# Short-row weights and tables laid out with 16 KB per partition, the last up matrix in quarters, and every second unit of expert weights issued by ScalarE's queue

## What is computed

```python
def hierarchical_moe(h, wg_r, bg_r, we_r, be_r, w_gate, w_up, w_down):
    """Top-1 expert group, then top-2 experts inside it; SwiGLU experts."""
    ...
    def expert_block(args):
        xb, e = args
        a = jax.nn.silu(xb @ w_gate[e]) * (xb @ w_up[e])
        return a @ w_down[e]
```

## Time and profile before

| | us |
|---|---|
| median of three runs | 1203.53 |
| the profiled execution | 1203.57 |
| its span in the trace | 1201.8 |
| TensorE busy | 961.0 |
| VectorE busy | 212.3 |
| ScalarE busy | 140.9 |

### The profile page before, as it was taken

The page is one execution under the profiler, slowest core; times in us unless marked ns, Lnnn a source line. Parts: engine busy times, 40 slices in busy tenths (PEclk is TensorE's granted clock), DMA queues, the critical chain, the costliest instruction groups (busy, mean ns, idle before and its releaser), DMA issues.

```text
span 1201.8 us, 11705 instructions
## 1 busy us (share of the span) xinstructions
PE 961.0 (80%) x5158; PEld 409.9 (34%) x5158; DVE 212.3 (18%) x457; ACT 140.9 (12%) x263; POOL 10.2 (1%) x11
## 2 busy tenths in 40 slices
PE   8999999867676767685789999997676767676758
PEld 7655554221212222222236655532121212121312
DVE  3812332010101010100025541410000000000101
ACT  3411211000000000000021330110000000000001
POOL 0000010000000000000000000000000000000000
PEclk9999999987878887888899999997878887878879
DMA  9772498999999999999997327999999999999996
GB/s 341 227 303 105 157 417 355 429 428 427 428 428 429 428 428 428 427 427 428 416 387 297 141 86 322 376 429 428 429 426 427 428 429 427 428 428 428 429 420 269
DMA packets 63237, 447.29 MB, mean 372 GB/s; under 512 B 13136, under 2 KB 13392, under 8 KB 40656
## 3 DMA queue, kind: packets, MB, share of 16 engines
q1 hardware_dynamic: 63184, 446.49, 90.0%
HBM read 445.43 MB, written 1.05 MB: 372 GB/s over the span
## 4 chain that ended last, share of the span: by engine, by line
DMA 50%; PE 47%; DVE 1%; ACT 1%; issue 0%; SPq 0%; DVEq 0%
PE psum L568 18%; DMA ring<-in_w_up 13%; PE psum L918 11%; DMA wide<-in_w_down 10%; DMA wide<-in_w_gate 10%; DMA ring<-in_w_down 5%; DMA wide<-in_w_up 5%; DMA ring<-in_w_gate 5%; PE psum L915 5%; PE psum L978 5%; PE psum L516 1%; PE psum L504 1%; DMA ring<-in_w_in_ab 1%; PE psum L992 1%; PE psum L636 0%
## 5 line engine op out<-in xcount | busy, mean ns | idle before, releaser
L568 PE MATMUL psum<-ring,mixed 128*32 128x512 f32 x1664 | 406.0, 712 | 125.5 <-DMA ring<-in_w_up 59.0
L568 PE MATMUL psum<-wide,mixed 128*32 128x512 f32 x1376 | 394.6, 709 | 101.2 <-DMA wide<-in_w_gate 61.9
L568 PEld LDWEIGHTS psum<-ring,mixed 128*32 128x32 f32 x1664 | 91.5, 128 | 331.7 <-issue 163.8
L568 PEld LDWEIGHTS psum<-wide,mixed 128*32 128x32 f32 x1376 | 87.2, 127 | 256.5 <-issue 116.3
L918 PE MATMUL psum<-ring,wide 128*128 128x512 f32 x320 | 140.5, 593 | 1.3 <-DVE wide L830 1.3
L918 PEld LDWEIGHTS psum<-ring,wide 128*128 128x128 f32 x320 | 59.7, 191 | 69.5 <-issue 67.8
L504 PE MATMUL psum<-y_sb,spread 128*128 128x512 f32 x144 | 67.2, 607 | 2.8 <-ACT y_sb L695 1.4
L752 DVE TENSOR_TENSOR mixed<-psum,sig 128x512 f32<-128x512 f32 x16 | 16.9, 1058 | 280.7 <-PE psum L568 280.7
L516 PEld LDWEIGHTS psum<-sel,h 128*128 128x128 f32 x528 | 60.5, 192 | 17.0 <-issue 15.1
L516 PE MATMUL psum<-sel,h 128*128 128x128 f32 x528 | 64.3, 279 | 1.7 <-DVE sel L728 1.7
L678 ACT COPY mixed<-psum 128x512 f32<-128x512 f32 x34 | 19.7, 586 | 344.7 <-PE psum L516 344.7
(11 more groups left out here) (252 smaller groups left out, 505.4 us busy)
## 6 DMA issues: line engine op xcount, KB each, us to landing
ring<-in_w_down SPq DMA_DIRECT2D x38, 2048.0 KB, 34.8
ring<-in_w_up SPq DMA_DIRECT2D x36, 2048.0 KB, 37.8
wide<-in_w_gate SPq DMA_DIRECT2D x34, 2048.0 KB, 37.2
ring<-in_w_gate SPq DMA_DIRECT2D x30, 2048.0 KB, 30.6
wide<-in_w_up SPq DMA_DIRECT2D x28, 2048.0 KB, 27.1
wide<-in_w_down SPq DMA_DIRECT2D x24, 2048.0 KB, 35.5
ring<-in_w_in_ab SPq DMA_DIRECT2D x8, 2048.0 KB, 14.3
ring<-in_w_in_cd SPq DMA_DIRECT2D x6, 2048.0 KB, 20.5
```

Of the source, the lines that this page charges most:

```text
L568: mm = pe.matmul(psum[slots, out + n, :], inp[:, c, slots], slot(layer, unit)[:, at + 512 * n:at + 512 * (n + 1)], start=c == 0, stop=c == ...
```

## The change

The input weights, output weights, quartered matrices and small tables are rearranged before the launch, so that every 2 MB unit is read as one 16 KB row per partition, and all small tables but two gains (and `positions`) as one array `tables` of 1188 floats per partition. Quad 7's up matrix joins `QUARTERED`. Units 11, 13, 15 ... 83 of each layer's experts leave SP's stream and are issued from ScalarE's, by `load_more`, after the sigmoid, after the copy of the transposed routing weights and after the output copy; for this ScalarE's loop over the quads is written out. Units 84 to 95 stay with SP. The diff's core:

```diff
-N_SMALL = 19
+N_SMALL = 2
...
-QUARTERED = ((0, 0), (QUADS - 1, 2))
+QUARTERED = ((0, 0), (QUADS - 1, 1), (QUADS - 1, 2))
...
+        def load_unit(eng, layer, n, dst_cols, src):
+            if unit_free(layer, n):
+                eng.wait_ge(S["unit_used"], unit_free(layer, n))
+            eng.dma_start(dst_cols(slot(layer, n)), src).then_inc(unit_landed[unit_place(layer, n)], 16)
...
+            elif (quad, matrix) in QUARTERED:
+                load_unit(eng, layer, expert_unit(layer, u), lambda s: s, t["quarters"][layer, matrix, j])
...
+        def from_act(u):
+
+            return len(PLACES_MOE) <= u < n_moe - PER_QUAD and u % 2 == 1
...
             def load_in(layer, n):
-                b = BLOCKS[layer][n]
-                src = w_in[layer][0].rearrange("(c p) n -> p c n", p=P)[:, :, b * 512:(b + 1) * 512]
-                load_unit(layer, n, lambda s: s.rearrange("p (c n) -> p c n", c=KC), src)
+                load_unit(sp, layer, n, lambda s: s, t["w_in"][layer * UNITS_IN[0] + n])
...
+            sp.dma_start(tables[:, :], t["tables"]).then_inc(S["lb_landed"], 16)
...
                 for u in range(10, n_moe):
-                    load_expert_unit(layer, u)
+                    if not from_act(u):
+                        load_expert_unit(sp, layer, u)
...
+            def load_more(i, matrices):
+
+                if over:
+                    return
+                freed = moe_base(layer) + i * PER_QUAD + matrices * TILE
+                for u in range(n_moe):
+                    if from_act(u) and freed - TILE < unit_free(layer, expert_unit(layer, u)) <= freed:
+                        load_expert_unit(act, layer, u)
+
             def act_quad(i, last=False):
                 wait_matrices(act, layer, rnd, i, 1)
                 nc.scalar.activation(sig, psum[:, GATE, :], ACT.Sigmoid).then_inc(m["sig_ready"], 1)
+                load_more(i, 1)
                 keep_gathered(i + (n17 + 2))
                 act.wait_ge(m["turned"], n16 + i + 1)
                 nc.scalar.copy(actT, psum[:, GATE, :].rearrange("p (c s) -> p c s", c=FC))
                 nc.scalar.copy(spread, psum[:, UP, 0:TC * P].rearrange("p (c s) -> p c s", c=TC)).then_inc(m["actT_ready"], 1)
+                load_more(i, 2)
...
                 nc.scalar.copy(y_sb[:, 0:512], psum[:, YB, :]).then_inc(m["y_ready"], 1)
+                load_more(i, 3)
```

More of the change, by code:

```diff
@@ L331, in heads, with load_expert_unit @@
             return a.rearrange("p c (h d) -> p c h d", h=HEADS)
+        def load_unit(eng, layer, n, dst_cols, src):
+            if unit_free(layer, n):
+                eng.wait_ge(S["unit_used"], unit_free(layer, n))
+            eng.dma_start(dst_cols(slot(layer, n)), src).then_inc(unit_landed[unit_place(layer, n)], 16)
+        def load_expert_unit(eng, layer, u):
+            quad, matrix, j = u // PER_QUAD, u // TILE % MATRICES, u % TILE
+            w, rows = (("w_gate", KC), ("w_up", KC), ("w_down", FC))[matrix]
+            if u == n_moe - 1:
+                n = expert_unit(layer, u)
+                eng.wait_ge(S["unit_used"], unit_free(layer, n))
+                for b, signal in enumerate((S["half_landed"], unit_landed[unit_place(layer, n)])):
+                    eng.dma_start(slot(layer, n)[:, b * HALF:(b + 1) * HALF],
+                                 t["quarters"][layer, 2, j, :, b * HALF:(b + 1) * HALF]).then_inc(signal, 16)
+            elif (quad, matrix) in QUARTERED:
+                load_unit(eng, layer, expert_unit(layer, u), lambda s: s, t["quarters"][layer, matrix, j])
+            else:
+                src = t[w][layer, quad * TILE + j].rearrange("(p c) n -> p (c n)", c=rows)
+                load_unit(eng, layer, expert_unit(layer, u), lambda s: s, src)
@@ L346, in load_expert_unit @@
[L346 to L364, removed]
@@ L413, in _ @@
+            for which, name in enumerate(("ret_gnorm", "hgrn_onorm")):
+                sp.dma_start(retg[:, which, :], t[name].rearrange("a h d -> a (h d)").broadcast_to([P, GROUP_W])).then_inc(
+                    S["small_landed"], 16)
             for layer in range(2):
@@ L697, in moe_act @@
             keep_gathered(n17 + 1, first=not over)
[L698 to L701, removed]
+            if over:
+                with act.Fori(0, QUADS) as i:
+                    act_quad(i)
+            else:
+                for i in range(QUADS):
+                    act_quad(i, last=i == QUADS - 1)
         def clear_outputs(layer):
@@ L1794, in _, with laid_out, quarters @@
             add_experts(dve, 1)
[L1797 to L1800, removed]
+PARAMS = ["x", "norm_ffn", "ret_gnorm", "hgrn_onorm", "w_gate", "w_up", "w_down"]
+def laid_out(inputs):
+    put = {n: np.ascontiguousarray(inputs[n]) for n in PARAMS}
+    w_in, w_out = [], []
+    for layer, pair in enumerate(("ab", "cd")):
+        for b in BLOCKS[layer]:
+            block = inputs["w_in_" + pair][0][:, b * 512:(b + 1) * 512]
+            w_in.append(block.reshape(KC, P, 512).transpose(1, 0, 2).reshape(P, UNIT))
+        for half in OUT_ORDER[layer]:
+            rows = inputs["w_out_" + pair][0][512 * half:512 * (half + 1)]
+            w_out.append(rows.reshape(4, P, D).transpose(1, 0, 2).reshape(P, UNIT))
+    put["w_in"], put["w_out"] = np.stack(w_in), np.stack(w_out)
+    def quarters(w, rows):
+        e = w.reshape(TILE, P, 4, rows // 4, -1)
+        return e.transpose(2, 1, 0, 3, 4).reshape(4, P, UNIT)
+    last = slice(N_EXPERTS - TILE, N_EXPERTS)
+    put["quarters"] = np.stack([np.stack([quarters(inputs["w_gate"][l, :TILE], KC), quarters(inputs["w_up"][l, last], KC),
+                                          quarters(inputs["w_down"][l, last], FC)]) for l in range(2)])
+    final = put["quarters"][:, 2, 3].reshape(2, P, TILE, 2, 512)
+    put["quarters"][:, 2, 3] = final.transpose(0, 1, 3, 2, 4).reshape(2, P, UNIT)
+    every = lambda a: np.broadcast_to(a.reshape(1, -1), (P, a.size))
+    by_row = lambda a: a.reshape(2, KC, P, -1).transpose(2, 0, 1, 3).reshape(P, -1)
+    tables = {
+        "lbt": inputs["hgrn_lb_logits"].reshape(3, HEADS, P).transpose(2, 0, 1).reshape(P, -1),
+        "dg": np.concatenate([every(inputs["diff_qnorm"]), every(inputs["diff_knorm"])], 1),
+        "dlam": np.concatenate([every(inputs["diff_lam_" + n]) for n in ("q1", "k1", "q2", "k2")], 1),
+        "subln": every(inputs["diff_subln"]),
+        "gcol": by_row(inputs["norm_ffn"]),
+        "rw": by_row(np.concatenate([inputs["router_group_w"], inputs["router_expert_w"]], 2)),
+        "rb": every(np.concatenate([inputs["router_group_b"], inputs["router_expert_b"]], 1)),
+    }
+    put["tables"] = np.concatenate([tables[name] for name, _ in TABLES], 1)
+    put["positions"] = inputs["positions"].reshape(TC, P).T
+    return {f"in_{n}": np.ascontiguousarray(a) for n, a in put.items()}
```

71 lines of the change are left out of this document (24 added, 47 removed).

## The result

The changed kernel takes 1211.77 us (median of 7 runs, 1209.23 to 1214.33) where before takes 1203.53 (7 runs, 1201.48 to 1206.88): ratio 1.0062, 95% interval 1.0046 to 1.0079. It is slower, by 0.6%. The forecast was 1208.3. The profiled execution of the changed kernel took 1211.0 us, with a span of 1209.2: 7.4 us over before's 1201.8.

A forecast was written before the change was run, and what follows sets the result against it. DMA at 428 GB/s was taken to bound the expert stages, TensorE the mixers. From 1203.57 us, start -2.5, stream's late start +6.0 and tail +1.2 gave 1208.3 us, range 1199.5 to 1215.5.

The forecast's parts named there:

- Part 2: Expert stream's start: SP's first load moves 3.84 us later in each layer, some comes back; +6.0 us.
- What I gave back: Expert stream's start: landings recover some of the 3.84 us delay, leaving 3.1 us in layer 0, 2.9 in layer 1.
- Part 1: Start, up to 12.16 us: 16 KB rows land unit 0 sooner and the clock stays up; -2.5 us.
- Sum -2.5: Start: 0.6 us from unit 0's longer rows plus 1.9 us from the granted clock; bounds -0.4 to -2.8.
- rival D: Start: the layout gives nothing, part 1 falls out, 1210.8 us; inside the forecast, no separate chance.
- Part 3: Tail with the last up matrix in quarters: +0.3 and +0.8 us, together +1.2 rounded up (-2.1 to +4.5).
- about the middle: Tail: last half at T+19.6, between T+18.0 at full and T+21.3 at half clock; T is the last up unit's landing.
- the 7 us of matmuls taken from behind T: Tail: matmuls no longer behind the last up unit's landing (T) give nothing, since data is the next thing late.
- A: Shared expert stretch: two queues hide the cost per row, 9.6 us, 1198.7 us, faster; chance 0.13.
- C: Expert stages: ScalarE's units land too late, slots free too late and the stream rests; 1220 us, chance 0.10.
- cushion: Expert stream: 3.5 units, 17 us, of slots left at each freeing, so ScalarE's lag costs nothing.
- B: Stream's late start made up elsewhere: tail -2.1 at full clock, start gives 2.8; 1204.7 us, no difference, chance 0.27.

The follow-up runs named there:

- twelve fillers: Changed kernel with all expert loads on SP, plus twelve filler matmuls before the waits for the last down matrix's second and third quarters; 1211.64 us, ratio 1.0053.
- ScalarE from 15: Changed kernel with only units 11 and 13 of each layer back in SP's stream, ScalarE issuing from unit 15; 1203.36 us, ratio 0.9993.
- before, again: The kernel before the change, unaltered, profiled a second time; 1205.23 us in one run.
- three fillers: Changed kernel with all expert loads on SP, plus three filler matmuls before the waits for the last down matrix's second and third quarters; 1200.90 us, ratio 0.9966.

## Why the prediction was right, point by point

**Part 2, who issues and when: right, +6.0 against +6.5.** SP's first load moved by 3.83 us (191.61 less 187.78) as read in the order, ScalarE's came at its sigmoid, and the stream passed nearly all of it on. Measured +3.94 and +2.52, forecast 3.1 and 2.9. Over all traces D has the mean 404.6 where unit 11 goes out early (eleven traces, 22 stretches, 403.9 to 406.0) and 407.8 where it goes out late (three traces, 407.7 to 407.9): 3.3 a layer, 6.6. What I gave back, 0.7 and 0.9 us by the order of landings, was a little too much: the missing bytes in the windows are 3.87 and 3.5 us. D itself scatters by 2 us where unit 11 goes out early, and before's layer 1, with 405.35, lies in its upper half; why it scatters no run shows. Single landings scatter as well: my 7.75 us for a load from rest was 9.4 in this execution (191.61 to 201.0) and 7.45 in the next.

**Part 1, start: mis-sized, -2.5 forecast, 0 measured in the pair.** The term "Sum -2.5" had 0.6 us for the rows, which are 0.4 (11.59 against 12.0) and 0 in the profiled execution, and 1.9 for the clock, which is not the layout's (a fall there costs 1.69, 12.29 less 10.60). I inferred from two idles that a shorter one leaves the clock alone. The runs show no such line: with the first projection at 11.97 (the run with twelve fillers) and 12.15 it fell, at 12.05 (ScalarE from 15) and 12.12 (before, again) it did not. TensorE's timeline has the idle in brackets. Twelve fillers, where it fell:

```profile
11.97 2.46 PE L916 MATMUL psum<-wide,ring 128*128 128x256 f32 x6 [1.90 <-DMA ring<-in_w_in]
```

before, again, where it did not:

```profile
12.12 2.18 PE L915 MATMUL psum<-wide,ring 128*128 128x256 f32 x9 [2.57 <-DMA ring<-in_w_in_ab]
```

So the longer idle kept the clock. The Trainium skill ("TensorE: Matmul & The Clock Gate", section "What's actually happening") says of a kernel's first matmuls that the monitor behind the clock runs free of the kernel, so that the point of a change varies from run to run. These traces agree, for falls too (0.50 in before's first trace, 1.00 in its second, at the same place), and by that rule the gain was a matter of chance in either kernel. Of rival D the price, 1210.8, was nearest to the time.

**Part 3, up in quarters: +1.2 forecast, +1.0 in the pair,** +0.6 over all traces. The forecast was S of 19.6 in both layers, "about the middle" between two clocks. Their mean is 19.6, but that the middle was met is in part luck, since the layers differ: 18.6 in layer 0 (18.1 in five traces, 19.8 in two), 20.7 in layer 1, in the profile with half clock over the last quarters (16 records in 3.45 us at 1193.71). That the 7 us of matmuls taken from behind T give nothing is right: 4.29 and 2.12 us of waiting for down quarters stand there instead.

**Rivals.** A, queues that hide the cost per row: 428 GB/s as before and D of 404.1 with two queues from unit 15; it did not happen. The rule quoted there from the Trainium skill ("DMA: Bandwidth & Descriptors", section "Issuing engines are not separate DMA queues"), that DMAs of different issuers interleave on the same engines, agrees with this trace. C, slots freed too late: it did not happen either, the share stays at 1.01. Unit 11 landed at 209.7 (forecast 208.4) and was wanted at 211.0. Units now land in pairs, and TensorE waits longer at the head of a matrix; its timeline:

```profile
229.21 1.06 PE L553 MATMUL psum<-wide,mixed 128*32 128x512 f32 x1 [8.73 <-DMA wide<-in_w_gate]
...
248.79 1.06 PE L553 MATMUL psum<-ring,mixed 128*32 128x512 f32 x1 [5.41 <-DMA ring<-in_w_up]
```

These are longer waits than the 3.85 us of the earlier trace rows, one matrix every 19.58 us, four units of 4.90: the rate is the same, so the stream had a cushion; that it is 17 us no run measures. B, made up elsewhere: no, the start gave nothing and the tails 1.0 us more.

The median rose by 8.2 us where 4.8 were forecast. The time is 3.5 us over the forecast: 2.5 of part 1, 0.5 of part 2, less 0.2 of part 3 (all rounded), and 0.8 that lie between the profiled execution and the median (1211.0 and 1211.77).

**Left open.** What decides whether the clock falls at the start; why layer 1's tail has late quarters and half clock more often than layer 0's; and how much of the 3.0 us between the medians of the runs without and with three fillers (1203.86 and 1200.90) is the clock, of which S shows 1.5. The traces can't settle the last: the profiled execution with three fillers took 1204.34 us, 3.4 over its own median.

## What to carry to other kernels

When loads are handed to a second engine, look at what stands ahead of the first one on that engine: in a stream that is bound by bytes, a load that is due when nothing else is under way must stay with the engine that waits for nothing else. Here all later ones could move without gain or harm. Where a stage ends in short work between landings, a filler that fits between two landings kept the clock here and was paid back; too long for the gap, it becomes the bound itself, so take its price from a row.

## What the hardware showed that I had not expected

- Two queues shared evenly. SP's units of the changed kernel that are issued at 191.61 and 195.04 land 9.4 and 15.8 us later, at 201.0 and 210.8: 9.8 us apart, where one queue has 4.90. ScalarE's two land at 209.7 and 219.4, 9.7 apart, and the two queues move 428 GB/s together. From issue to landing, the first alone:

```profile
DMA to landing us min/median/max: 9.4/9.4/9.4
```

SP's second with ScalarE's first (14.6):

```profile
DMA to landing us min/median/max: 14.6/15.2/15.8
```

- The granted clock at one place of one kernel is not the same from execution to execution: 0.50 for 3.4 us behind before's first projection in one trace, 1.00 in the next, and then 0.50 at the routing. Of the fourteen traces four fall at the first place, six at the second, four at neither.
- Four transfers of 512 KB behind one another brought unit 0 at 12.7 to 12.9 (three traces), one of 2 MB at 11.25 to 12.02.
